# S5 batch: one y tile over four row groups and four column groups, single-buffered in PSUM; compact complex products, padded by GpSimd and ScalarE; skip term on TensorE

## The reference

```python
def s5_mixer(h, w_in, log_dt, lam_re, lam_im, b_re, b_im, c_re, c_im, d_skip, w_glu):
    u = h @ w_in
    dt = exp(log_dt)[:, None];  mag = exp(lr * dt)
    ab_r, ab_i = mag * cos(li * dt), mag * sin(li * dt)
    f_r, f_i = ...                       # (ab - 1) / lambda, complex
    bb_r = f_r * br - f_i * bi;  bb_i = f_r * bi + f_i * br
    # per chunk of 128 tokens: x[t] = ab * x[t-1] + bb @ u[t]   (complex scan)
    y = einsum(x_r, cr) - einsum(x_i, ci)
    y = y + d_skip * u
    g = gelu(y)
    val, gate = split(g @ w_glu, 2)
    return val * sigmoid(gate)
```

## Time and profile before

| | |
|---|---|
| time, median of 3 runs | 1326.34 us (1326.29 to 1328.05) |
| profiled execution: span | 1324.4 us |
| around the span, against that median | 1.9 us |
| PE busy | 1296.3 us, 98% |
| POOL busy | 1006.1 us, 76% |
| ACT busy | 682.9 us, 52% |
| DVE busy | 637.0 us, 48% |
| mean granted clock of PE | 0.999 |

### The profile page before, as it was taken

How to read it: one execution, slowest core, us unless ns; L and a number is a source line. 1 busy time by engine, 2 the same in 40 slices (tenths; PEclk the granted TensorE clock), 3 DMA queues, 4 the chain that set the end, 5 groups by cost and what they waited for, 6 DMA issues and landing times.

```text
span 1324.4 us, 27666 instructions
## 1 busy us (share of the span) xinstructions
PE 1296.3 (98%) x10976; PEld 1247.4 (94%) x10976; DVE 637.0 (48%) x1163; ACT 682.9 (52%) x944; POOL 1006.1 (76%) x793
## 2 busy tenths in 40 slices
PE   6999999999999999999999999999999999999999
PEld 6889999999988889999999978999999999999998
DVE  8994465555555748455565574211113455311112
ACT  7725643444666756443457565434446566543342
POOL 1327888888777659888887794988887766988885
PEclk9999999999999999999999999999999999999999
DMA  6305675545535235555454532555554433555530
GB/s 269 129 33 181 169 250 191 185 172 181 191 134 185 101 126 183 178 188 188 172 178 160 193 128 96 192 192 179 174 185 167 160 126 120 187 178 187 190 127 32
DMA packets 33879, 217.07 MB, mean 164 GB/s; under 512 B 3683, under 2 KB 7428, under 8 KB 8196
## 3 DMA queue, kind: packets, MB, share of 16 engines
q1 hardware_dynamic: 30096, 211.14, 45.1%
q10 hardware_dynamic: 3700, 4.75, 1.4%
HBM read 213.26 MB, written 2.62 MB: 163 GB/s over the span
## 4 chain that ended last, share of the span: by engine, by line
PE 85%; DVE 6%; ACT 6%; issue 2%; POOL 1%; DMA 0%; DVEq 0%; SPq 0%; ACTq 0%; POOLq 0%
PE up L1568 19%; PE up L1569 18%; PE up L1570 18%; PE acc L1568 7%; PE acc L1570 6%; PE acc L1569 6%; DVE opnd L972 2%; PE side L1795 2%; PE up L1703 1%; PE acc L1761 1%; ACT w_hi L503 1%; ACT opnd L641 1%; PE side L1576 1%; PE up L1834 1%; PE acc L1933 0%
## 5 line engine op out<-in xcount | busy, mean ns | idle before, releaser
L413 POOL TENSOR_TENSOR w_lo<-ring,w_hi 128x512 fp32r<-128x512 f32 x748 | 955.4, 1311 | 235.7 <-ACT w_hi L503 231.8
L1568 PE MATMUL up<-opnd,w_hi 128*128 128x256 f32 x2064 | 592.3, 287 | 3.7 <-DVE opnd L972 1.5
L1569 PE MATMUL up<-opnd,w_lo 128*128 128x256 f32 x2064 | 583.9, 283 | 0.0
L1570 PE MATMUL up<-opnd,w_hi 128*128 128x256 f32 x2064 | 583.8, 283 | 0.0
L503 ACT ACTIVATE w_hi<-ring 128x2048 fp32r<-128x2048 f32 x188 | 358.9, 1910 | 264.4 <-PE up L1570 202.7
L1568 PEld LDWEIGHTS up<-opnd,w_hi 128*128 128x128 f32 x2064 | 395.6, 192 | 16.1 <-issue 13.1
L1569 PEld LDWEIGHTS up<-opnd,w_lo 128*128 128x128 f32 x2064 | 395.8, 192 | 1.3 <-issue 1.0
L1570 PEld LDWEIGHTS up<-opnd,w_hi 128*128 128x128 f32 x2064 | 395.7, 192 | 0.0
L1568 PE MATMUL acc<-opnd,w_hi 128*128 128x256 f32 x784 | 223.0, 284 | 1.2 <-DVE x L1218 1.2
L1569 PE MATMUL acc<-opnd,w_lo 128*128 128x256 f32 x784 | 221.8, 283 | 0.0
L1570 PE MATMUL acc<-opnd,w_hi 128*128 128x256 f32 x784 | 221.8, 283 | 0.0
(11 more groups left out here) (296 smaller groups left out, 1421.3 us busy)
## 6 DMA issues: line engine op xcount, KB each, us to landing
ring<-in_stream SPq DMA_DIRECT2D x197, 1024.0 KB, 4.9
bias_rows<-mix ACTq DMA_DIRECT2D x1, 1536.0 KB
mix<-in_s_b SPq DMA_DIRECT2D x1, 1024.0 KB, 5.6
x<-in_x SPq DMA_DIRECT2D x1, 1024.0 KB, 7.7
mix<-in_s_c SPq DMA_DIRECT2D x1, 1024.0 KB, 11.7
mix<-bias_rows ACTq DMA_DIRECT2D x1, 1024.0 KB, 5.4
out_x<-x SPq DMA_DIRECT2D x8, 128.0 KB, 1.7
mix<-in_p ACTq DMA_DIRECT2D x2, 256.0 KB, 3.4
```

Of the source, the lines that this page charges most:

```text
L413: ins = nc.gpsimd.tensor_tensor(w_l[:, cols], ring[:, r, cols], w_h[:, cols].bitcast(f32), ALU.subtract)
L1568: MM(o, l_hi, r_hi, start=start, stop=False, skip_group_check=True)
L1569: MM(o, l_lo, r_hi, start=False, stop=False, skip_group_check=True)
L1570: return MM(o, l_hi, r_lo, start=False, stop=stop, skip_group_check=True)
```

## The change

- A batch is now one y tile: its four pairs stand on four row groups of `s5_in` and four column groups of `s5_out`. `acc` holds one batch of inputs instead of two (`s5_in(n)` waits for the products of n-1). The count of matmuls in `s5_in` and `s5_out` stays the same.
- The skip term is a full diagonal matmul on PE for all 8 tiles (in `s5_out`); DVE's `s5_output` is gone, and ACT copies tiles 0 to 3 out of PSUM (`s5_raw`). POOL makes the first four diagonals, ACT the last four.
- The complex products are written compactly (two instructions on 128 partitions instead of four on 64). POOL copies B, and C at both steps, into their padded places (and takes the compact form of C, formerly ACT's); ACT copies the product of B into `s_in`.
- The turns of table 1 move from DVE (`turns(1)`) to ACT (`s5_turns(1)`) with `less_whole(1)` on DVE behind `s5_scan(0)`; `s5_tables(1)` on ACT then stands behind that.
- x is loaded ahead of B. The parts of `w_in` and of `glu` slot 0 are cut otherwise around the S5 matmuls on PE.

```diff
+            pool.wait_ge(dma["par"], 16)
+            for j in range(4):
+                c.up(nc.gpsimd.tensor_scalar(s_dg[:, j], ident, pcol("dskip", j, 1), None, ALU.mult), "s5_diag")
...
+            pool.wait_ge(dma["s5_c"], 16)
+            for h in range(2):
+                part, cols = own(s_craw, h)
+                c.up_and_wait(nc.gpsimd.tensor_copy(own(s_cn, h)[0], part[:, :, :, cols]), "s5_cn")
+            c.up_and_wait(nc.gpsimd.memset(ring[:, RING - 1], 0.0), "s5_bt_clear")
+            c.wait("s5_bn", 2)
+            for h in range(2):
+                part, cols = own(s_bt, h)
+                c.up_and_wait(nc.gpsimd.tensor_copy(part[:, :, :, cols], own(s_bn, h)[0]), "s5_bt")
+            def padded(step):
+                c.wait("s5_cc", 2)
+                for h in range(2):
+                    part, cols = own(s5_cm[:, :, step], h)
+                    c.up_and_wait(nc.gpsimd.tensor_copy(part[:, :, :, cols], own(s_cc[step], h)[0]), "s5_cm")
+            padded(0)
+            padded(1)
...
             decay(0)
+            s5_turns(1)
             s5_tables(1)
             c.wait("k0_ps")
...
+            act.wait_ge(sem("s5_cm"), 4)
+            s5_turns(2)
+            decay(1)
+            s5_raw(0)
+            s5_turns(3)
+            decay(2)
...
-            def complex_product(dst0, dst1, src, f0, f1, op0, op1, name):
+            def complex_product(dst, src, f0, f1, op0, op1, name):
                 g0, g1 = (w[:, f].unsqueeze(1).unsqueeze(3).broadcast_to([P, 2, PAIRS, GDIM]) for f in (f0, f1))
                 also(TTo(s_t0, src, g0, ALU.mult))
                 step(TTo(s_t1, src, g1, ALU.mult))
-                for h in range(2):
-                    t0, t1 = own(s_t0, h)[0], own(s_t1, h)[0]
-                    (d0, cols), (d1, _) = own(dst0, h), own(dst1, h)
-                    c.up(TTo(d0[:, :, cols], t0[:, 0], t1[:, 1], op0), name)
-                    c.up(TTo(d1[:, :, cols], t1[:, 0], t0[:, 1], op1), name)
+                c.up(TTo(dst[:, 0], s_t0[:, 0], s_t1[:, 1], op0), name)
+                c.up(TTo(dst[:, 1], s_t1[:, 0], s_t0[:, 1], op1), name)
...
             evacuate(0)
-            turns(1)
...
-                if n in (0, 2):
+                if n in (2, 4):
                     evacuate(1 + n // 2)
                 s5_scan(n)
-                if n in (1, 2):
+                if n < 3:
                     less_whole(n + 1)
-                if n == 4:
-                    evacuate(3)
+                if n == 0:
+                    evacuate(1)
...
                 s5_back(n)
-                if 2 <= n < 6:
-                    s5_output(n - 2)
...
-                if n >= 2:
+                if n:
                     c.wait("s5_prod", 2)
                 for s in range(2):
-                    for i in range(2):
-                        for r in range(2):
-                            for e in range(2):
-                                q, m = 2 * b + e, 2 * M + i
+                    for r in range(2):
+                        for q in range(4):
+                            rows = slice(32 * q, 32 * q + 32)
+                            ins = MM(acc[:, q, r * P:r * P + P], s_in[rows, s, r, n * P:(n + 1) * P],
+                                     sq[rows, n, s * P:(s + 1) * P], ...)
```

More of the change, by code:

```diff
@@ L578, in _ @@
                 c.up(A(ssm_x[:, m], x[:, m], ACT.Copy, scale=gain("ssm", m)), "ssm_ready")
-            act.wait_ge(dma["s5_c"], 16)
+            for m in range(KT // 2):
+                c.up(A(sq[:, m], x[:, m], ACT.Square), "sq_ready")
+            c.wait("s5_bt_ps", 2)
+            b_ps = acc[:].rearrange("p (r a) (b c) -> p r (a b) c", r=2, c=32)
             for h in range(2):
-                part, cols = own(s_craw, h)
-                c.up(A(own(s_cn, h)[0], part[:, :, :, cols], ACT.Copy), "s5_cn")
-            for r in range(2):
-                c.up(A(s_bt[:, r], b_ps[r], ACT.Copy, scale=1.0 - 2.0 * r), "s5_bt")
-            for m in range(KT):
+                part, cols = own(b_ps, h)
+                c.up(A(own(s_bn, h)[0], part[:, :, :, cols], ACT.Copy), "s5_bn")
+            for m in range(KT // 2, KT):
                 c.up(A(sq[:, m], x[:, m], ACT.Square), "sq_ready")
             s5_tables(0)
+            act.wait_ge(sem("s5_ab_clear"), 1)
+            c.wait("s5_abn", 2)
+            for h in range(2):
+                part, cols = own(s_ab, h)
+                c.up(A(part[:, :, :, cols], own(s_abn, h)[0], ACT.Copy), "s5_ab")
             c.wait("eps")
@@ new lines, in s5_out @@
+                if n == 0:
+                    c.wait("s5_diag", 4)
+                    c.wait("k0_sb", 4)
+                    c.wait("s5_cm", 2)
+                if n in (2, 3, 4, 5):
+                    pe.wait_ge(sem("s5_raw"), n - 1)
+                if n == 4:
+                    c.wait("s5_diag_late", 4)
+                if n >= 6:
+                    pe.wait_ge(sem("s5_gelu"), n - 1)
+                MM(o, skip(n), sq[:, n], start=True, stop=False, skip_group_check=True)
+                MM(o[:, 0:P], s_k0[:, n], sq[:, n, 0:P], start=False, stop=False, skip_group_check=True)
@@ L1805, in _ @@
             s5_k0()
+            s5_in(2)
             o = whole_bank(S + 2)
             whole_part(S + 2, o, front)
-            s5_in(2)
+            s5_out(0)
             s5_in(3)
-            c.wait("s5_cm", 4)
-            c.wait("k0_sb", 4)
-            s5_out(0)
             whole_part(S + 2, o, rest)
@@ L1839, in _ @@
             o = whole_bank(S)
-            gelu_part(o, range(4))
+            gelu_part(o, range(2))
+            s5_out(5)
+            gelu_part(o, range(2, 5))
+            s5_out(6)
+            gelu_part(o, range(5, 6))
             s5_out(7)
-            gelu_part(o, range(4, KT))
+            gelu_part(o, range(6, KT))
             for m in range(1, KT):
```

169 lines of the change are left out of this document (75 added, 94 removed).

## The result

The changed kernel took 1329.61 us (median of 15 runs, 1328.52 to 1330.64); the kernel before, run beside it, 1327.15 (15 runs, 1326.28 to 1328.12). The ratio is 1.002, with a 95% interval of 1.0013 to 1.0027. The forecast was 1329.4, which is 1326.3 and 3.1 on top; between the two medians the change costs 2.5, because before's median over 15 runs lies 0.8 above that 1326.3. The profiled execution took 1329.26, with a span of 1327.5, 3.1 more than before's 1324.4.

The account below looks back on a forecast made before the run. DVE was taken to set the loop and PE the last 7.3 us behind it, before PE's long three-pass run. Terms -2.2 + 3.8 + 1.05 + 0.4 = +3.1 on 1326.3 gave 1329.4, range 1323.5 to 1335 (8 in 10).

Parts of the forecast that it names:

- Head if nothing collides: Start of kernel: without POOL collisions, three DVE products end at 26.5, PE reaches s5_in(0) at 28.3, less_whole(1) ends at 39.0.
- POOL's copies take turns: Head: POOL copies (1.05 each) alternate with DVE's products, third product at 31.2 instead of 26.5, s5_in(0) 3.8 late.
- The chain on ACT: Between less_whole(1) and scan(1): tables, k0 copies, turns(2) and decay(1) take 9.9 us and hold DVE 3.3.
- The half clock: Head: after PE idles 3.8 us its clock falls to the 1.2 GHz level, so s5_in(0) takes 1.05 more.
- Four row groups: PE per batch: s5_in on four groups takes 1.05 instead of 2.0; PE savings in the loop are worth nothing.
- no faster than two: Rival: four row groups run like two, s5_in(0) and (1) 1 us longer each; 1331.4 with turns, 1326.5 without; chance 0.07.
- Loop: Scan(1) to end of back(7): 51.5 instead of 52.3, gaining 0.46 from evacuate(3) and 0.3 from waits ahead of products(6).
- Tail: From back(7) to the first three-pass product: 4.4 instead of 7.3, plus 0.4 added for PE's clock.
- just in time: Behind the tail: POOL's low part of glu+2 needs 5.3, starting 0.5 behind slot glu+1, whose products take 5.8.
- a copy does not take turns: Rival, head: one-input POOL copies do not slow DVE, 3.8 and 1.05 fall away; about 1324.5 or 1323.5; chance 0.36.
- copies at the pace of the sums: Rival, head: POOL copies take 2.5 us per 1024, six turns adding 9; about 1335 to 1338; chance 0.13.
- the change nets to nothing: Rival, whole kernel: head gain and ACT hold cancel, 1326.3; contained in the edges of the first two rivals.

Follow-up runs that it names:

- e1: Changed kernel with POOL's B copies (and the C copies behind them) held until DVE's third product is done; 1326.51 us, ratio 0.9998.
- e6: Changed kernel with POOL's B copies written as memsets of zeros to the same places at the same time; 1327.03 us, ratio 0.9999.
- e3: Changed kernel with less_whole(1) on DVE moved from behind scan(0) to between the products of tiles 0 and 1; 1324.24 us, ratio 0.9983.
- e2: Changed kernel with ACT's decay(1) moved ahead of the k0 copies and turns(2), right behind tables(1); 1326.90 us, ratio 1.0.
- e10: The same kernel as e4, run again for a second profile; 1331.21 us.
- e8: Changed kernel with the matmuls of s5_in(3) to s5_in(7) issued over two row groups in turn; 1329.67 us, ratio 1.0025.
- e4: Changed kernel with the matmuls of s5_in(3) to s5_in(7) reordered so that neighbours share a row group; 1333.38 us, ratio 1.0048.
- e5: Changed kernel with the edits of e1 and e3 together; 1322.76 us, ratio 0.997.
- e7: e5 with POOL's sum(0) between the C copies of step 0 and those of step 1; 1322.11 us, ratio 0.9962.
- e12: Changed kernel with the one-row-group order of e4 for s5_in(6) and s5_in(7) alone; 1330.09 us, ratio 1.0022.

## Why the prediction was right, step by step

The time was right to 0.2 us, and part of that is luck. By the landmarks two errors of 0.7 cancel: the first three-pass product moved by 2.4 (106.72 to 109.12) where 3.1 was forecast, and 0.7 was lost behind it, where nothing was. And the 1326.3 on which the forecast stood is 0.8 below the median of 15 runs of the kernel before.

- **Head if nothing collides:** right. Forecast for `s5_in(0)` 28.3; e1, which has no collision but that of the C copies of 14.40, 28.14, with TensorE just done with its own work, as forecast. A product takes 3.7 (20.01 to 23.73 in e6) where I took 3.8.
- **POOL's copies take turns:** right in kind, a little over in size. Forecast was 15.0 to 31.2 for the three products, measured 15.24 to 30.39. I had 4.7 for it and it was 4.0: the first of the six copies ran ahead of DVE's first product, and the other five lengthened one instruction each by 0.71 to 0.84. The price of one copy was right (1.065 against 1.05). e1 takes four of the five away and the third product comes 3.12 earlier; e6 shows with the same addresses and times that it is the reading. The Trainium skill ("GPSIMD Engine Reference", Key points), which names VectorE instructions with two SBUF inputs as those that contend, agrees with that (2.06 for 1.22), and the products of tile 0 in e1, which read PSUM, keep their 1.22 and 1.21 (29.45 to 31.8) beside POOL's copies of 29.61 to 33.9.
- **The chain on ACT:** right. From the end of `less_whole(1)` to scan(1) the forecast was 9.9, and it is 9.85 (43.04 to 52.89). That the forecast hold (3.3) equals the idle time ahead of scan(1) (3.25) is chance: it left out the 1.07 ahead of products(2). Scan(1) could have started at about 48.9 (an estimate: back(0) ends at 46.22, and e3 needs 2.69 from there), so the chain held it by 4.0 in all. e2 and e3 shorten the chain from either end and the time falls by 2.7 and 5.4.
- **The half clock:** right in size, one step off in place. I put 1.05 on `s5_in(0)`; that ran in 1.17, and the quarter behind it in 3.64 instead of 1.99. On the path that is 0.96 (4.67 against 3.71). It is the term with the least hold on the time: the profiles of e2 and e10 have the same gap and do not pay it.
- **Four row groups:** 1.17 against my 1.05, 0.1 a batch. Neighbours in pairs of groups take 1.72, in one group 2.82, so the rival "no faster than two" falls. That TensorE's savings in the loop are worth nothing is only half right. e8 gives 0.55 a batch back and the time stays; e4 gives 1.65 back in five batches and the median rises by 3.8, by the reading above, because the saving is the slack that hides stretches at the lower clock. The saving of the column groups (`s5_out` 1.95 for 3.67) was not taken back in any run.
- **Loop:** 51.9 against 51.5. From scan(3) to scan(5) it is 15.6 instead of 16.0, which is the forecast gain of evacuate(3) (0.46). The other forecast gain, 0.3 for waits ahead of products(6), is not there: from scan(5) to scan(6) it was 7.61 and is 7.60.
- **Tail:** 4.3 against 4.4. The 0.4 that I added for the clock was worth nothing there. The clock did fall (`s5_out(7)` 3.13 instead of 1.95, then 2.43 for eight records), but `w_low` on DVE ends as late, and e3, whose last `s5_out` ran at full clock, has the same 4.3.
- **Behind the tail:** the term that was missing. From the first three-pass product to the end it was 1217.7 and is 1218.4, in e3 and e5 too (1218.5 each). I had called POOL's low part of glu+2 just in time. It starts at 109.65, 0.53 behind the first three-pass product, where before it was 0.33 behind (107.05 and 106.72), and by 124 DVE's norms are later by about the same 0.2 against that start. The other 0.5 comes in far behind the stage: POOL's last four low parts start at 1309.14 instead of 1306.03, 3.1 later. I did not trace it.

The rivals: that a copy does not take turns is excluded by e1 and e6, copies at the pace of the sums by the 1.065. That the change nets to nothing was close (the measured ratio is 1.002), since gains and holds of some microseconds each do cancel here; e2, e3 and e1 show that any one of the holds removed brings the kernel back to the time before or below it.

## What to carry to other kernels

Work taken off a busy engine gains little more than slack where another engine sets the pace; look instead at what had to move to make room for it, because copies given to an "idle" GpSimd and tables put behind a later ACT chain both came back on DVE's path. Price a hold together with what it can trigger: taking away 1.4 us of lost DVE time gave 2.4 in one profile and 2.6 between the medians, since the gap on TensorE became shorter and the lower clock did not follow it; with the long gap it followed in six profiles of eight. And when two holds stand in a row, remove the one at the head of the longest chain first (5.4 us for a move of one instruction), then look again, since the next wait (POOL's sum) may take most of the second gain.

## What the runs showed of the hardware that was not expected

- The turn-taking is mutual but not even. Beside DVE's products a POOL copy takes 1.5 to 2.0 instead of 1.065. Beside `less_whole(1)` POOL's four copies took 1.0 longer and it kept its own 1.22 (e5), and POOL's sum took 2.12 instead of 1.26 (e3), while a scan beside two copies went from 2.34 to 3.92 (e7).
- A granted clock at the lower level lengthens only what is issued in it, and which instruction that is differs from run to run. Behind the same 2.38 us of idle time the last `s5_out` took 3.13 in the changed kernel and 1.95 in e12, and behind 3.18 and 3.25 the quarter of the head kept 1.99 in e2 and e10. So the length of the gap alone does not tell whether the clock falls.
- The order of independent small matmuls alone changes their pace: 32 records of 32 rows take 1.17 us over four row groups in turn, 1.72 over two, 2.82 with neighbours in one group.
